# Last rows of a hybrid decoder step: gates in the one-hot rows, residual rows added by TensorE, sample rows spread over 64 partitions, tiles normed and stored one by one

## The chip, the core and the metric

The kernel runs on one core of a Trainium2 chip. The metric is the device time of one launch in microseconds. A core has TensorE (PE in the profile, its weight loads PEld), VectorE (DVE), ScalarE (ACT), GpSimd (POOL) and SyncE (SP), which here issues the large transfers; they run side by side, each in the order of its own queue, and wait for each other on semaphores.

## What is computed

One inference step of a decoder of two layers over 256 prompt rows and 8 sample rows of 1024 numbers, all in f32. The last sublayer is a mixture of eight experts, of which each row uses two, and the layer ends with a norm of each row:

```python
y = jnp.zeros_like(x)
for e in range(N_EXPERTS):
    y = y + swiglu(x, w_gu[e], w_down[e]) * combine[..., e:e + 1].astype(x.dtype)
...
hp = layer_norm(ALPHA * hp + fp, ln_g[i, 1], ln_b[i, 1])
hs = layer_norm(ALPHA * hs + fs, ln_g[i, 1], ln_b[i, 1])
```

`y_prompt` (256 x 1024) and `y_sample` (8 x 1024) are the last `hp` and `hs`; six states are further outputs, written long before the end.

## The kernel before

The rows stand in three tiles: tiles 0 and 1 are the 256 prompt rows, 128 to a tile on the partitions, and tile 2 is the 8 sample rows. The experts are run one after the other as jobs of up to 128 gathered rows. A job has 42 weight slots of 1 MB: SyncE loads a slot into `raw`, ScalarE rounds it to `high` (L352), VectorE subtracts to get `low` (L357), and TensorE multiplies with both (L2132 to L2136 for gate and up, L2161 and L2167 for down). In the loop over slots, `i` is the slot's number in its job.

A job's result of 128 rows is copied from PSUM banks 4 and 5 into `ysb`, half by ScalarE (L1017) and half by VectorE (L1631). All jobs but the last store it to DRAM. `acc` holds, for each tile, the residual (ALPHA times the row before the mixture); in the last expert VectorE adds the rows of each token's first and second expert that came from earlier jobs (L1602), gathered from DRAM and multiplied by the gate. The rows that come from the last job don't go through DRAM: `final_oh` (L1638) is a one-hot matrix of tokens by seats, TensorE transposes it (L2187), VectorE copies it into `final_ohT` (L1627), and after the last slot TensorE multiplies it with `ysb` (L2199), for the tiles in the order 2, 0, 1, two halves of 512 columns each, into the banks that `final_bank` names. All of these are f32 matmuls; the trace has two records (passes) for each.

VectorE then, for each tile in that order, adds the product times the gate to `acc` (L1662, one operation for each half), takes the statistics of each half (bn_stats, L1666) and combines them (bn_aggr, L1668). When all three are done, ScalarE takes Ln and Exp for 1/sqrt(var + eps) of all tiles (L1028, L1030), while VectorE runs (x - mean) * g over each tile (L1677) and then * rstd + b (L1682). Each tile of L1682 releases a store by SyncE (L515 for the sample rows, L517 for the prompt tiles of 512 KB each). GpSimd waits for the stores.

`Steps` is a counter with a semaphore: `step(instruction)` raises it, `step.wait()` waits for all that was counted.

Of the kernel before, what the change touches and what calls it, by code (L numbers as in the profile page):

```python
# [7 lines left out]
D = 1024  # L8
# [54 lines left out]
def hybrid_step(nc, x_prompt, x_sample, state_gdn_S, state_gdn_conv, state_sconv, ln_g, ln_b, gdn_w_in,  # L63
# [8 lines left out]
    with ExitStack() as ctx:  # L72
# [176 lines left out]
        gate_bm = place("gate_bm", [128, 3], at=region + 90 * D + 1568)  # L249
        zeros = place("zeros", [128, 256], at=zeros_at)  # L250
# [212 lines left out]
        def _(sp_):  # L463
# [48 lines left out]
            for tt in (2, 0, 1):  # L512
                sp_.wait_ge(y_ready, 1 + (0 if tt == 2 else tt + 1))
                if tt == 2:
                    sp_.dma_start(y_sample[:, 0, :], acc[0:NS, 2, :]).then_inc(y_out, 16)  # L515
                else:
                    sp_.dma_start(y_prompt[0, 128 * tt:128 * tt + 128, :], acc[:, tt, :]).then_inc(y_out, 16)  # L517
# [3 lines left out]
        def _(pool):  # L521
# [164 lines left out]
            pool.wait_ge(y_out, 48)  # L686
# [8 lines left out]
        def _(act):  # L695
# [331 lines left out]
            act.wait_ge(var_ready, 2)  # L1027
            act.activation(rstd_n[:, :], moments[:, :, 1], ACT.Ln, bias=eps[:, 1:2]).then_inc(log_ready, 1)  # L1028
            act.wait_ge(log_ready, 1)
            act.activation(rstd_n[:, :], rstd_n[:, :], ACT.Exp, scale=-0.5).then_inc(rstd_ready, 1)  # L1030
# [3 lines left out]
        def _(dve):  # L1034
# [569 lines left out]
            def expert(job, last, first=False):  # L1604
# [6 lines left out]
                for i in range(EXPERT_SLOTS):  # L1611
# [10 lines left out]
                    if i == EXPERT_SLOTS - 3:  # L1622
                        if not last:
                            gathered(job + 1)
                        else:
                            dve.wait_ge(ohT_psum, 1)
                            dve.tensor_copy(final_ohT[:, :], bank[2][:, 0:N]).then_inc(ohT_ready, 1)  # L1627
# [8 lines left out]
                    if last and i == 2:  # L1636
                        for tt in range(3):
                            ins = dve.tensor_scalar(final_oh[:, tt, :], seat[:, :], seat_b[:, tt:tt + 1], None, ALU.is_equal)  # L1638
                        ins.then_inc(oh_ready, 1)
                    if last and i in (20, 22, 24):  # L1640
# [15 lines left out]
            for i, tt in enumerate((2, 0, 1)):  # L1656
                p = 128 if tt < 2 else NS
                step.wait()
                for g in range(2):
                    dve.wait_ge(yrow_psum, 2 * i + g + 1)  # L1660
                    at = acc[0:p, tt, 512 * g:512 * g + 512]
                    step(dve.scalar_tensor_tensor(at, bank[final_bank(tt) + g][0:p, :], gate_ab[0:p, 1, tt:tt + 1], at,  # L1662
                                                  ALU.mult, ALU.add))
                step.wait()
# [563 lines left out]
```

## Time and profile before

| | us |
|---|---|
| median of 3 runs (1565.75 to 1566.30) | 1566.19 |
| profiled execution | 1567.19 |
| its span (first to last record on the core) | 1565.5 |
| PE busy | 1531.1 |
| DVE busy | 1279.2 |
| ACT busy | 1039.8 |

Times in the trace count from the start of the span. A group of instructions is given by line, engine, operation and tiles (out<-in), with its count, its busy time and the mean time of one. "idle before" is the time in which the engine did nothing just before them, with what ended it.

### The profile page before, as it was taken

Reading aid. Unit: us, or ns where it says so; the run is one execution under the profiler, and the core shown is the slowest. Engines: PE = TensorE matmul, PEld = TensorE weight load, DVE = VectorE, ACT = ScalarE, POOL = GpSimd, SP = SyncE. Lnnn points to the kernel's source line nnn. Section 1 sums busy time; section 2 is a strip of 40 time slices with the busy share of each in tenths; the row PEclk is TensorE's granted clock in tenths of the full one; section 3 lists DMA queues with packets and bytes.
Section 4 is the critical chain, followed back from the end, with each engine's and each line's share of the span. In section 5 each row is a group of like instructions: output and inputs, shape, how many; then the busy total and the mean of one; then the engine's idle time right before and its main releaser. Section 6 shows DMA issues by size and latency. Waiting matters only on the chain.

```text
span 1565.5 us, 23507 instructions
## 1 busy us (share of the span) xinstructions
PE 1531.1 (98%) x8904; PEld 1342.8 (86%) x8904; DVE 1279.2 (82%) x1285; ACT 1039.8 (66%) x967; POOL 104.2 (7%) x155
## 2 busy tenths in 40 slices
PE   8999999999999999999999999999999999999995
PEld 7899999999999998888888888888888888888883
DVE  6886555787446868999889889889889889889897
ACT  5874335676335447778778778778778778777772
POOL 3106000011000011000000000000000000003100
PEclk9999999999999999999999999999999999999998
DMA  9747605698545539999999999999999999999990
GB/s 290 241 138 275 236 15 188 202 300 283 188 162 190 188 110 373 376 380 383 386 376 374 386 375 373 389 373 378 389 373 371 391 373 377 387 378 373 411 399 28
DMA packets 227447, 476.67 MB, mean 304 GB/s; under 512 B 9692, under 2 KB 69100, under 8 KB 227081
## 3 DMA queue, kind: packets, MB, share of 16 engines
q1 hardware_dynamic: 216040, 435.66, 76.6%
q0 software_dynamic: 11344, 40.12, 7.5%
q8 instruction: 45, 0.74, 0.2%
q14 instruction: 18, 0.15, 0.0%
HBM read 449.74 MB, written 26.24 MB: 304 GB/s over the span
## 4 chain that ended last, share of the span: by engine, by line
PE 89%; DVE 5%; ACT 4%; issue 2%; DMA 0%; DVEq 0%; SPq 0%; ACTq 0%
PE bank L2136 13%; PE bank L2132 12%; PE bank L2133 12%; PE bank L392 12%; PE bank L2161 11%; PE bank L398 6%; PE bank L2167 5%; PE bank L1996 2%; DVE low L357 2%; ACT high L352 2%; PE bank L2144 2%; PE bank L1817 1%; DVE xf L1542 1%; PE bank L2001 1%; PE bank L1833 1%
## 5 line engine op out<-in xcount | busy, mean ns | idle before, releaser
L357 DVE TENSOR_TENSOR low<-raw,high 128x2048 fp32r<-128x2048 f32 x405 | 920.7, 2289 | 147.9 <-ACT high L352 145.3
L352 ACT ACTIVATE high<-raw 128x2048 fp32r<-128x2048 f32 x405 | 775.5, 1918 | 299.1 <-PE bank L2136 92.1
L2132 PE MATMUL bank<-high,xgh 128*128 128x512 f32 x896 | 353.8, 395 | 0.4 <-DVE xgl L1548 0.4
L2133 PE MATMUL bank<-high,xgl 128*128 128x512 f32 x896 | 349.5, 390 | 0.0
L2136 PE MATMUL bank<-low,xgh 128*128 128x512 f32 x896 | 241.3, 391 | 0.9 <-DVE low L357 0.5
L2136 PEld LDWEIGHTS bank<-low,xgh 128*128 128x128 f32 x896 | 167.5, 188 | 39.9 <-DVE low L357 4.6
L2132 PEld LDWEIGHTS bank<-high,xgh 128*128 128x128 f32 x896 | 168.3, 188 | 34.5 <-issue 0.5
L2133 PEld LDWEIGHTS bank<-high,xgl 128*128 128x128 f32 x896 | 168.3, 188 | 33.9
L392 PE MATMUL bank<-xhb,high 128*128 128x266 f32 (+1 forms) x752 | 158.0, 292 | 0.0
L392 PE MATMUL bank<-xlb,high 128*128 128x266 f32 (+1 forms) x752 | 155.0, 287 | 0.0
L2161 PE MATMUL bank<-high,hth 128*128 128x512 f32 x448 | 139.5, 392 | 0.0
L2161 PE MATMUL bank<-high,htl 128*128 128x512 f32 x448 | 138.2, 390 | 0.0
L392 PEld LDWEIGHTS bank<-xhb,high 128*128 128x128 f32 x752 | 119.1, 191 | 2.0 <-issue 1.8
L2167 PE MATMUL bank<-low,hth 128*128 128x512 f32 x448 | 119.9, 389 | 0.0
L392 PEld LDWEIGHTS bank<-xlb,high 128*128 128x128 f32 x752 | 118.9, 191 | 0.0
L398 PE MATMUL bank<-xhb,low 128*128 128x266 f32 (+1 forms) x752 | 100.4, 286 | 0.0
L2161 PEld LDWEIGHTS bank<-high,htl 128*128 128x128 f32 x448 | 84.1, 188 | 17.7
L2167 PEld LDWEIGHTS bank<-low,hth 128*128 128x128 f32 x448 | 84.1, 188 | 17.6
L2161 PEld LDWEIGHTS bank<-high,hth 128*128 128x128 f32 x448 | 82.9, 188 | 16.4
L398 PEld LDWEIGHTS bank<-xhb,low 128*128 128x128 f32 x752 | 95.7, 189 | 0.1
L1009 ACT ACTIVATE sgx<-bank 128x512 f32<-128x512 f32 x56 | 33.6, 600 | 39.4 <-PE bank L2136 39.3
L679 POOL TENSOR_TENSOR flag<-flag 128x1 f32<-128x1 f32 x1 | 3.4, 3352 | 838.2 <-DMA tok<-ysb 838.2
(417 smaller groups left out, 1554.8 us busy)
## 6 DMA issues: line engine op xcount, KB each, us to landing
raw<-in_moe_w_gu_dram SPq DMA_DIRECT2D x224, 1024.0 KB, 6.5
raw<-in_moe_w_down_dram SPq DMA_DIRECT2D x112, 1024.0 KB, 6.6
raw<-in_ffn_w_gu_dram SPq DMA_DIRECT2D x22, 1024.0 KB, 5.1
raw<-in_gdn_w_in_dram SPq DMA_DIRECT2D x16, 1024.0 KB, 8.7
tok<-zeros POOLq DMA_DIRECT2D x26, 512.0 KB, 18.1
raw<-in_sc_w_in_dram SPq DMA_DIRECT2D x12, 1024.0 KB, 5.0
raw<-in_ffn_w_down_dram SPq DMA_DIRECT2D x11, 1024.0 KB, 4.9
s<-in_state_gdn_S_dram POOLq DMA_DIRECT2D x8, 512.0 KB, 6.5
```

Of the source, the lines that this page charges most:

```text
L352: eng.activation(high[:, n % SPLIT, :], raw[:, n % RAW, :], ACT.Copy).then_inc(high_ready, 1)
L357: eng.tensor_tensor(low[:, n % RAW, :], raw[:, n % RAW, :], high[:, n % SPLIT, :].bitcast(F32), ALU.subtract).then_inc(low_ready, 1)
L392: pe.matmul(out[t], wh[:, k, f[t]], act_[:, k, :], start=k == 0 and act_ is act_h, stop=False)
L398: last = pe.matmul(out[t], wl[:, k, f[t]], act_h[:, k, :], start=False, stop=k == KT - 1)
L1009: act.activation(sgx[:, u % 2, :], bank[2 * (u % 2)][:, :], ACT.Silu).then_inc(sgx_ready, 1)
L1996: pe.matmul(bank[d][:, 0:N], wh[:, k, 128 * d:128 * d + 128], act_[:, f + k, :], start=f + k == 0 and act_ is hh, stop=False)
L2132: pe.matmul(out, xgh[:, 4 * kh + k, :], wh[:, k, :], start=kh + k == 0, stop=False)
L2133: pe.matmul(out, xgl[:, 4 * kh + k, :], wh[:, k, :], start=False, stop=False)
L2136: last = pe.matmul(out, xgh[:, 4 * kh + k, :], wl[:, k, :], start=False, stop=kh == 1 and k == 3)
L2144: last = pe.transpose(bank[6 + u % 2][:, 128 * q:128 * q + 128], hx[:, u % 2, 128 * q:128 * q + 128], idn)
L2161: pe.matmul(bank[4 + g][:, :], src[:, u % 2, hs], wh[:, k, 512 * g:512 * g + 512], start=u + kh + k == 0 and src is hth, stop=False)
L2167: last = pe.matmul(bank[4 + g][:, :], hth[:, u % 2, hs], wl[:, k, 512 * g:512 * g + 512], start=False, stop=u == UNITS - 1 and kh + k == 2)
```

## The change

The gate of the last job's expert is multiplied into the one-hot matrix `final_oh`, so the product of L2199 comes out gated. TensorE adds the residual: a matmul of the identity with `acc` goes into the same PSUM bank ahead of the product. VectorE takes statistics and the centred rows straight from PSUM. The order of the tiles becomes 0, 1, then the sample rows. The 8 sample rows of 1024 are laid out as 64 partitions of 128: `row_win` and `seat_win` are windows of 64 weight columns, shifted by one for each of eight blocks of 128 columns; eight matmuls of each kind build the rows in bank 0, and sixteen more spread the norm's g and b in bank 1. `same_row` sums a row's eight partitions, once for the mean and once for the variance. ScalarE takes Ln and Exp for each tile by itself. Tile 0 is finished and stored first, then the sample rows, then tile 1 in two halves of 512 columns.

```diff
--- before.py
+++ after.py
@@ -247,6 +247,16 @@
         part_a = place("part_a", [128, 3, EX], at=tab_at + 6048)
         seat_b = place("seat_b", [128, 3], at=region + 90 * D + 1536)
         gate_bm = place("gate_bm", [128, 3], at=region + 90 * D + 1568)
+        seat_win = place("seat_win", [128, 72], at=tab_at + 480)
+        row_win = place("row_win", [NS, 72], at=tab_at + 768)
+        same_row = place("same_row", [HEADS * NS, HEADS * NS], at=tab_at + 1056)
+        row_of = place("row_of", [HEADS * NS, NS], at=tab_at + 1312)
+        sstats = place("sstats", [HEADS * NS, 6], at=tab_at + 1344)
+        smom = place("smom", [HEADS * NS, 2], at=tab_at + 1376)
+        smean = place("smean", [HEADS * NS, 1], at=tab_at + 1408)
+        srstd = place("srstd", [HEADS * NS, 1], at=tab_at + 1440)
+        srows = place("srows", [HEADS * NS, 128], at=tab_at + 1472)
+        srow_g = place("srow_g", [HEADS * NS, 128], at=region + 24 * D)
         zeros = place("zeros", [128, 256], at=zeros_at)
         tok = nc.dram_tensor("tok", [JOBS + 2, CAP, D], F32).ap()
         tok_rows = tok.rearrange("j p d -> (j p) d")
@@ -509,12 +519,14 @@
                     down(UNITS - 1)
                 sp_.wait_ge(tiles_ready, 1)
                 sp_.reg_load(tiles, rounds_i[0:1, 0:1])
-            for tt in (2, 0, 1):
-                sp_.wait_ge(y_ready, 1 + (0 if tt == 2 else tt + 1))
-                if tt == 2:
-                    sp_.dma_start(y_sample[:, 0, :], acc[0:NS, 2, :]).then_inc(y_out, 16)
-                else:
-                    sp_.dma_start(y_prompt[0, 128 * tt:128 * tt + 128, :], acc[:, tt, :]).then_inc(y_out, 16)
+            sp_.wait_ge(y_ready, 1)
+            sp_.dma_start(y_prompt[0, 0:128, :], acc[:, 0, :]).then_inc(y_out, 16)
+            sp_.wait_ge(y_ready, 2)
+            sp_.dma_start(y_sample[:, 0, :].rearrange("b (d c) -> (b d) c", c=128), srows[:, :]).then_inc(y_out, 16)
+            for g in range(2):
+                gs = slice(512 * g, 512 * g + 512)
+                sp_.wait_ge(y_ready, 3 + g)
+                sp_.dma_start(y_prompt[0, 128:256, gs], acc[:, 1, gs]).then_inc(y_out, 16)
 
 
         @block.gpsimd
@@ -683,7 +695,7 @@
             for tt in (2, 0, 1):
                 gather_rows(1, tt, rows_b, b_in[tt])
 
-            pool.wait_ge(y_out, 48)
+            pool.wait_ge(y_out, 64)
             pool.wait_ge(hist_out, 48)
             pool.wait_ge(tail_out, 32)
             for i in range(2):
@@ -1024,10 +1036,15 @@
                 expert(job, False)
             expert(final, True)
             act.preload_act_table_set("natural_log_exp_and_others")
-            act.wait_ge(var_ready, 2)
-            act.activation(rstd_n[:, :], moments[:, :, 1], ACT.Ln, bias=eps[:, 1:2]).then_inc(log_ready, 1)
-            act.wait_ge(log_ready, 1)
-            act.activation(rstd_n[:, :], rstd_n[:, :], ACT.Exp, scale=-0.5).then_inc(rstd_ready, 1)
+            for tt in range(2):
+                act.wait_ge(var_ready, 2 + tt)
+                act.activation(rstd_n[:, tt:tt + 1], moments[:, tt, 1:2], ACT.Ln, bias=eps[:, 1:2]).then_inc(log_ready, 1)
+                act.wait_ge(log_ready, 1 + tt)
+                act.activation(rstd_n[:, tt:tt + 1], rstd_n[:, tt:tt + 1], ACT.Exp, scale=-0.5).then_inc(rstd_ready, 1)
+            act.wait_ge(yrow_psum, 8)
+            act.activation(srstd[:, :], bank[5][0:HEADS * NS, 1:2], ACT.Ln, bias=eps[0:HEADS * NS, 1:2]).then_inc(log_ready, 1)
+            act.wait_ge(log_ready, 3)
+            act.activation(srstd[:, :], srstd[:, :], ACT.Exp, scale=-0.5).then_inc(rstd_ready, 1)
 
 
         @block.vector
@@ -1624,7 +1641,11 @@
                             gathered(job + 1)
                         else:
                             dve.wait_ge(ohT_psum, 1)
-                            dve.tensor_copy(final_ohT[:, :], bank[2][:, 0:N]).then_inc(ohT_ready, 1)
+                            step(dve.tensor_copy(final_ohT[:, :], bank[2][:, 0:N]))
+                            step(dve.tensor_copy(seat_win[:, 0:64].rearrange("p (b d) -> p b d", d=8)[:, :, 7:8],
+                                                 bank[2][:, NP:N].rearrange("p (b o) -> p b o", o=1)))
+                            step.wait()
+                            dve.tensor_scalar(same_row[:, :], same_row[:, :], 1.0 / 8, None, ALU.mult).then_inc(ohT_ready, 1)
                     if i == EXPERT_SLOTS - 1:
                         dve.wait_ge(slot_used, done + (MOE0 + i + 1))
                         dve.wait_ge(y_stored, job * 16 + 16)
@@ -1635,8 +1656,18 @@
                         residual_rows((i - 12) // 4)
                     if last and i == 2:
                         for tt in range(3):
-                            ins = dve.tensor_scalar(final_oh[:, tt, :], seat[:, :], seat_b[:, tt:tt + 1], None, ALU.is_equal)
+                            ins = dve.tensor_scalar(final_oh[:, tt, :], seat[:, :], seat_b[:, tt:tt + 1], gate_ab[:, 1, tt:tt + 1],
+                                                    ALU.is_equal, ALU.mult)
                         ins.then_inc(oh_ready, 1)
+                    if last and i == 14:
+                        step(dve.memset(seat_win[:, :], 0.0))
+                        step(dve.memset(row_win[:, :], 0.0))
+                        step(dve.tensor_reduce(row_of[:, :], ident[0:64, 0:64].rearrange("p (b d) -> p b d", d=8), X, ALU.add))
+                        step.wait()
+                        step(dve.tensor_copy(row_win[:, 0:64].rearrange("p (b d) -> p b d", d=8)[:, :, 7:8],
+                                             ident[0:NS, 0:NS].rearrange("p (b o) -> p b o", o=1)))
+                        step(dve.tensor_copy(same_row[:, :].rearrange("p (b d) -> p b d", d=8),
+                                             row_of[:, :].rearrange("p (b o) -> p b o", o=1).to_broadcast([64, NS, 8])))
                     if last and i in (20, 22, 24):
                         tt = (2, 0, 1)[(i - 20) // 2]
                         p = 128 if tt < 2 else NS
@@ -1653,34 +1684,50 @@
                 expert(job, False)
             step.wait()
             expert(final, True)
-            for i, tt in enumerate((2, 0, 1)):
-                p = 128 if tt < 2 else NS
+
+            def row_moments(tt):
+                for g in range(2):
+                    dve.wait_ge(yrow_psum, 2 * tt + g + 1)
+                    step(dve.bn_stats(stats[:, tt, g, :], bank[final_bank(tt) + g][:, :]))
                 step.wait()
+                dve.bn_aggr(moments[:, tt, :], stats[:, tt, :, :].rearrange("p g s -> p (g s)")).then_inc(var_ready, 1)
+
+            def centred(tt):
+                dve.wait_ge(var_ready, 2 + tt)
                 for g in range(2):
-                    dve.wait_ge(yrow_psum, 2 * i + g + 1)
-                    at = acc[0:p, tt, 512 * g:512 * g + 512]
-                    step(dve.scalar_tensor_tensor(at, bank[final_bank(tt) + g][0:p, :], gate_ab[0:p, 1, tt:tt + 1], at,
-                                                  ALU.mult, ALU.add))
-                step.wait()
-                for g in range(2):
-                    step(dve.bn_stats(stats[:, tt, g, :], acc[:, tt, 512 * g:512 * g + 512]))
-                step.wait()
-                ins = dve.bn_aggr(moments[:, tt, :], stats[:, tt, :, :].rearrange("p g s -> p (g s)"))
-                if tt == 1:
-                    ins.then_inc(var_ready, 1)
-                else:
-                    step(ins)
-            step.wait()
-            dve.wait_ge(var_ready, 2)
-            dve.wait_ge(vec_in, 64)
-            for tt in (2, 0, 1):
-                step(dve.scalar_tensor_tensor(acc[:, tt, :], acc[:, tt, :], moments[:, tt, 0:1], vec_g[:, :],
-                                              ALU.subtract, ALU.mult))
-            step.wait()
+                    gs = slice(512 * g, 512 * g + 512)
+                    step(dve.scalar_tensor_tensor(acc[:, tt, gs], bank[final_bank(tt) + g][:, :], moments[:, tt, 0:1], vec_g[:, gs],
+                                                  ALU.subtract, ALU.mult))
+
+            def finished(tt, gs):
+                dve.scalar_tensor_tensor(acc[:, tt, gs], acc[:, tt, gs], rstd_n[:, tt:tt + 1], vec_b[:, gs],
+                                         ALU.mult, ALU.add).then_inc(y_ready, 1)
+
+            x_rows = bank[0][0:HEADS * NS, 0:128]
+            row_moments(0)
+            row_moments(1)
+            centred(0)
+            dve.wait_ge(yrow_psum, 5)
+            step(dve.bn_stats(sstats[:, :], x_rows))
+            step.wait()
+            dve.bn_aggr(smom[:, :], sstats[:, :]).then_inc(var_ready, 1)
             dve.wait_ge(rstd_ready, 2)
-            for tt in (2, 0, 1):
-                dve.scalar_tensor_tensor(acc[:, tt, :], acc[:, tt, :], rstd_n[:, tt:tt + 1], vec_b[:, :],
-                                         ALU.mult, ALU.add).then_inc(y_ready, 1)
+            finished(0, slice(0, D))
+            dve.wait_ge(yrow_psum, 7)
+            step(dve.tensor_copy(srow_g[:, :], bank[1][0:HEADS * NS, 0:128]))
+            step(dve.tensor_copy(smean[:, :], bank[4][0:HEADS * NS, 0:1]))
+            step.wait()
+            step(dve.tensor_tensor(smom[:, 0:1], smom[:, 0:1], smean[:, :], ALU.subtract))
+            step.wait()
+            dve.scalar_tensor_tensor(smom[:, 1:2], smom[:, 0:1], smom[:, 0:1], smom[:, 1:2], ALU.mult, ALU.add).then_inc(var_ready, 1)
+            centred(1)
+            step(dve.scalar_tensor_tensor(srows[:, :], x_rows, smean[:, 0:1], srow_g[:, :], ALU.subtract, ALU.mult))
+            step.wait()
+            dve.wait_ge(rstd_ready, 4)
+            dve.scalar_tensor_tensor(srows[:, :], srows[:, :], srstd[:, 0:1], bank[1][0:HEADS * NS, 128:256],
+                                     ALU.mult, ALU.add).then_inc(y_ready, 1)
+            for g in range(2):
+                finished(1, slice(512 * g, 512 * g + 512))
 
 
         @block.tensor
@@ -2192,12 +2239,40 @@
                 expert(job, False)
             expert(final, True)
             pe.wait_ge(ohT_ready, 1)
+
+            def residual(tt, g):
+                pe.matmul(bank[final_bank(tt) + g][:, :], idn, acc[:, tt, 512 * g:512 * g + 512], start=True, stop=False)
+
+            def weighted(tt, g):
+                pe.matmul(bank[final_bank(tt) + g][:, :], final_ohT[:, 128 * tt:128 * tt + 128], ysb[:, 512 * g:512 * g + 512],
+                          start=False, stop=True).then_inc(yrow_psum, 1)
+
+            for g in range(2):
+                residual(0, g)
             pe.wait_ge(y_sb, final * 2 + 4)
-            for i, tt in enumerate((2, 0, 1)):
-                n_tok = 128 if tt < 2 else NS
-                for g in range(2):
-                    pe.matmul(bank[final_bank(tt) + g][0:n_tok, :], final_ohT[:, 128 * tt:128 * tt + n_tok],
-                              ysb[:, 512 * g:512 * g + 512], start=True, stop=True).then_inc(yrow_psum, 1)
+            for g in range(2):
+                weighted(0, g)
+            for g in range(2):
+                residual(1, g)
+                weighted(1, g)
+
+            def sample_rows(out, win, rows):
+                for d in range(KT):
+                    last = pe.matmul(out, win[:, 7 - d:71 - d], rows[:, 128 * d:128 * d + 128], start=d == 0, stop=d == KT - 1)
+                return last
+
+            x_rows = bank[0][0:HEADS * NS, 0:128]
+            for d in range(KT):
+                ds = slice(128 * d, 128 * d + 128)
+                pe.matmul(x_rows, row_win[:, 7 - d:71 - d], acc[0:NS, 2, ds], start=d == 0, stop=False)
+                last = pe.matmul(x_rows, seat_win[:, 7 - d:71 - d], ysb[:, ds], start=False, stop=d == KT - 1)
+            last.then_inc(yrow_psum, 1)
+            pe.wait_ge(vec_in, 64)
+            sample_rows(bank[1][0:HEADS * NS, 0:128], row_win, vec_g[0:NS, :])
+            sample_rows(bank[1][0:HEADS * NS, 128:256], row_win, vec_b[0:NS, :]).then_inc(yrow_psum, 1)
+            for i in range(2):
+                pe.wait_ge(var_ready, 4 + i)
+                pe.matmul(bank[4 + i][0:HEADS * NS, 0:2], same_row[:, :], smom[:, :], start=True, stop=True).then_inc(yrow_psum, 1)
 
 
 # ---- launch: one core; inputs and outputs as the reference has them ----
```

## Rows read from the trace of the kernel before

**Rows 1.** The page: TensorE's busy share; granted clock in 40 slices.
```profile
PE 1531.1 (98%) x8904; PEld 1342.8 (86%) x8904; DVE 1279.2 (82%) x1285; ACT 1039.8 (66%) x967; POOL 104.2 (7%) x155
...
PEclk9999999999999999999999999999999999999998
```
**Rows 2.** The chain of waits from 1530 to 1566: start, us, what.
```profile
1542.32 1.90 PE bank L2199 x4
...
1544.24 0.75 DVE acc L1662
...
1549.59 1.42 DVE acc L1662 x2
...
1558.85 1.20 DVE acc L1682
```
**Rows 3.** The timeline of the end: start, us, engine, line, what, count.
```profile
1540.38 1.07 PE L2167 MATMUL bank<-low,hth 128*128 128x512 f32 x4
...
1541.58 0.69 DVE L1631 COPY ysb<-bank 128x512 f32<-128x512 f32 x1 [3.88 <-PE bank L2167]
...
1542.32 5.51 PE L2199 MATMUL bank<-ysb,final_ohT 128*8 128x512 f32 x12 [0.88 <-DVE ysb L1631]
...
1543.45 1.53 DVE L1662 SCALAR_TENSOR_TENSOR acc<-bank,gate_ab,acc 8x512 f32<-8x512 f32 x2 [1.19 <-PE bank L2199]
...
1558.88 1.53 SPq L517 DMA_DIRECT2D out_dram<-acc  x2
```
**Rows 4.** DMA from 1558 to 1566 in 40 slices: busy tenths, GB/s.
```profile
DMA  0072000039999989999991000000000000000000
GB/s 0 0 102 41 21 0 0 0 143 410 410 451 389 430 369 492 389 410 471 389 430 62 0 0 0 0 0 0 0 0 0 0 0 0 0 0 0 0 0 0
```
**Rows 5.** Groups by form, whole span: busy us, mean ns, idle before.
```profile
L2109 PE MATMUL bank<-onehot,xn 128*128 128x128 f32 x48 | 5.6, 277 | 0.0
...
L2109 PEld LDWEIGHTS bank<-onehot,xn 128*128 128x128 f32 x48 | 5.4, 192 | 0.5 <-DVE onehot L1508 0.5
...
L1666 DVE BATCH_NORM_STATS2 stats<-acc 128x6 f32<-128x512 f32 x6 | 3.9, 685 | 0.1
L1682 DVE SCALAR_TENSOR_TENSOR acc<-acc,rstd_n,vec_b 128x1024 f32<-128x1024 f32 x3 | 3.7, 1282 | 0.0
...
L1441 DVE BATCH_NORM_STATS2 quarters<-bank 128x6 f32<-128x256 f32 x8 | 3.0, 414 | 0.8 <-PE bank L2035 0.8
...
L1248 DVE SCALAR_TENSOR_TENSOR Vn<-bank,nbe,Vn 128x128 f32<-128x128 f32 x8 | 2.2, 342 | 2.0 <-PE bank L1891 2.0
...
L1668 DVE BATCH_NORM_AGGREGATE moments<-stats 128x2 f32<-128x12 f32 x3 | 0.6, 208 | 0.1
...
L1627 DVE COPY final_ohT<-bank 128x264 f32<-128x264 f32 x1 | 0.4, 426 | 0.0
...
L1533 DVE TENSOR_TENSOR most<-most 128x1 f32<-128x1 f32 x1 | 0.2, 159 | 0.0
...
L1028 ACT ACTIVATE rstd_n<-moments,eps 128x3 f32<-128x3 f32 x1 | 0.3, 297 | 9.1 <-DVE moments L1668 9.1
```
**Rows 6.** Waits in the last expert, 1425 to 1541: total, times, longest us.
```profile
DVE low L357 <- ACT high L352: 4.8, 10, 0.8
...
PEld bank L2136 <- DVE low L357: 0.4, 1, 0.4
```
**Rows 7.** VectorE's timeline in the last expert.
```profile
1469.33 2.29 DVE L357 TENSOR_TENSOR low<-raw,high 128x2048 fp32r<-128x2048 f32 x1 [0.42 <-ACT high L352]
1472.05 2.29 DVE L357 TENSOR_TENSOR low<-raw,high 128x2048 fp32r<-128x2048 f32 x1 [0.43 <-ACT high L352]
```
**Rows 8.** Windows: busy us of each engine, granted clock, DMA share, GB/s.
```profile
583.00:589.00 6.00, 5.64 (x49) 5.46 (x49) 4.43 (x24) 0.63 (x2) 2.66 (x3) 1.00 0.25 104
1547.50:1551.00 3.50, 0.34 (x1) 0.00 (x0) 3.40 (x6) 0.00 (x0) 0.00 (x0) 1.00 0.00 0
...
1552.40:1560.00 7.60, 0.00 (x0) 0.00 (x0) 7.47 (x7) 0.50 (x2) 0.00 (x0) 0.50 0.06 19
```

More of the change, by code:

```diff
@@ L1679, in _ @@
-            step.wait()
-            dve.wait_ge(rstd_ready, 2)
-            for tt in (2, 0, 1):
-                dve.scalar_tensor_tensor(acc[:, tt, :], acc[:, tt, :], rstd_n[:, tt:tt + 1], vec_b[:, :],
-                                         ALU.mult, ALU.add).then_inc(y_ready, 1)
+                    gs = slice(512 * g, 512 * g + 512)
+                    step(dve.scalar_tensor_tensor(acc[:, tt, gs], bank[final_bank(tt) + g][:, :], moments[:, tt, 0:1], vec_g[:, gs],
+                                                  ALU.subtract, ALU.mult))
@@ new lines, in _ @@
+            dve.wait_ge(rstd_ready, 2)
+            finished(0, slice(0, D))
+            dve.wait_ge(yrow_psum, 7)
+            step(dve.tensor_copy(srow_g[:, :], bank[1][0:HEADS * NS, 0:128]))
+            step(dve.tensor_copy(smean[:, :], bank[4][0:HEADS * NS, 0:1]))
+            step.wait()
+            step(dve.tensor_tensor(smom[:, 0:1], smom[:, 0:1], smean[:, :], ALU.subtract))
+            step.wait()
+            dve.scalar_tensor_tensor(smom[:, 1:2], smom[:, 0:1], smom[:, 0:1], smom[:, 1:2], ALU.mult, ALU.add).then_inc(var_ready, 1)
```

## The prediction

> **What bounds the kernel now.** I read the page first. TensorE is busy for 98% of the span, at the full clock in all of the 40 slices but the last [rows 1]: the kernel is bound by TensorE until its last microseconds, and those are another stage. The change acts almost only there. Then the chain of waits over the end [rows 2]: it runs through the copy into ysb and the first products of L2199, and from 1544.24 to 1560.05 through VectorE alone, so this stage is VectorE's chain, and the stores behind it. The timeline gives starts and spacings [rows 3]: twelve records of L2199 are six f32 matmuls of two passes, 0.43 us a pass; the first result is seen by VectorE at 1543.45, 1.13 us after its first pass began at 1542.32, that is 0.86 of streaming and 0.27 of drain and semaphore. The DMA view of the last 8 us (slices of 0.2) [rows 4]: the data of the two 512 KB stores, issued at 1558.88 and 1560.07, flow from 1559.6 without a hole to about 1562.35 at some 420 GB/s; the span ends at 1565.5, so 3.15 us follow the last byte.
>
> **The change in the expert stage.** It adds VectorE work in the last expert (i == 14: two memsets, a reduction, two copies, all on 72 columns or fewer; about 0.8 us at 0.16 for the smallest operation and 0.001 a column [rows 5]) and two instructions behind the copy into final_ohT, about 0.4 us. In the last expert VectorE waits 4.8 us in all for ScalarE's splits, and TensorE waited for VectorE's low half 0.4 us in all [rows 6]. The work of i == 14 falls at 1468.9, between two splits; the next two of them waited 0.42 and 0.43 us [rows 7], which takes up the 0.8. The other two fall in the 3.9 us in which VectorE waits for the last slot [rows 3]. I cost both at 0. Without that cover they cost at most 1.2 us, which goes into the range. The gate in final_oh is a second operation of the same instructions: 0. ScalarE's pairs (0.30 or less each [rows 5]) are small; the last is checked below.
>
> **The end, step by step.** TensorE first, since the change gives it far more to do ahead of VectorE.
>
> 1. *Residuals ahead of the product.* The four L2167 passes began at 1540.38 [rows 3], 0.23 apart, so the array is free at 1541.29. Two residual matmuls are four passes of 0.43, to 1543.01. ysb is there at 1542.28 [rows 3], so 0.7 us of them is on the path: the first product is seen at 1543.01 + 1.13 = 1544.14, the second at 1545.00.
> 2. *Second tile.* Residual and product alternate, 0.86 each: seen at 1546.72 and 1548.44, array free at 1548.17.
> 3. *Sample rows.* 16 f32 matmuls of 128 columns, 32 passes. The nearest row is L2109, 48 passes with 5.6 us busy, 0.117 each [rows 5]; a quarter of the 512-column pass is 0.107. The weights here have 64 columns, not 128; I take 0.110. 3.5 us, to 1551.7, seen at 1551.96.
> 4. *The norm's vectors spread over the rows.* 32 passes more, 3.5 us, to 1555.2. The first same_row product (two passes of two columns) is seen at about 1555.6.
>
>    A rule of the Trainium skill bears on the price of a pass. The rows show a load of 128 columns at 0.19 us of its own, and a period of 0.117 with it [rows 5]. "TensorE: Matmul & The Clock Gate", in its part on LDWEIGHTS, says that a load takes about its columns over 1.2 GHz, however many rows it has; as an estimate from it, 53 ns for 64 columns, which would hide under 0.107 of streaming: 6.8 us for the 64 passes by the page, 7.5 by the row.
>
> VectorE against this:
>
> 5. Tile 0: two bn_stats of 0.685 from 1544.14 and 1545.00, aggregate 0.21 [rows 5]: 1545.9. Tile 1: from 1546.72 and 1548.44, done at 1549.37; these waits are for TensorE. centred(0) is two operations in the form of L1662, 1.42 us a pair [rows 2]: 1550.85.
> 6. It waits for the sample rows until 1551.96. bn_stats of 128 columns: 512 cost 0.685 and 256 cost 0.414 [rows 5], so 0.28; aggregate 0.2: 1552.5. finished(0) is 1.28 [rows 5]: 1553.8. The first 512 KB store starts there, 6 us before VectorE ends, moves its data in 1.3 us and is out of the way. What comes later in VectorE's queue stands behind its next wait, yrow_psum 7, though centred(1) doesn't need it: idle from 1553.8 to 1555.6.
> 7. Copy of 128 columns 0.29 (0.16 for the smallest operation, 0.43 for 264 columns), copy of one column 0.15, two tiny operations at 0.16 each [rows 5]: 1556.4. centred(1) 1.42: 1557.85. Two operations on 64x128 at 0.34 each (L1248 [rows 5]): 1558.5. ScalarE's last pair needs the second same_row product (1556.9) and 0.6 us: 1557.5, hidden.
> 8. finished(1) in halves, again a pair at 1.42: 1559.9. Before, the last operation ended at 1560.05. Gain on VectorE: 0.15 us. It saved about 8.2 us (three gate pairs 1.42 x 3, the sample tile's two 1024-column operations 1.20 x 2, its statistics 1.5); that went into waits for TensorE of 0.7, 0.15, 0.8, 1.0, 1.1 and 1.8 us, 1.9 of small operations, and 0.6 because halves cost 1.42 where a whole cost 1.20.
> 9. *The stores.* The last is 256 KB, behind another 256, instead of 512 behind 512. Issued at 1559.2 and 1559.9, first data 0.7 us after issue as before, 0.63 us each at 420 GB/s: last byte at 1561.3 instead of 1562.35. Then the same 3.15 us: 1564.5. The 64 sample rows of 512 B are issued at 1558.5, ahead of both; the 32 KB before took under 0.7 us [rows 4].
>
>    By the rows the stores give 0.9 us beyond VectorE's 0.15. The Trainium skill, "DMA: Bandwidth & Descriptors", on where the 2 us of a transfer go, has it as 2.0 us fixed, mostly the receipt of the last write, plus bytes over 436 GB/s; as an estimate from it the last store lands 2.6 us after issue instead of 3.2, and the stores give 0.6. This trace has 3.15 us after the last byte, part of it the end of the program.
>
> Sum: 1564.5 against 1565.5, **1.0 us less**. The profiled execution took 1567.19 for its span of 1565.5; the median of the runs is 1566.19, so 1565.2.
>
> **Bounds of the unknown costs.** Pass: 0.107 gives -0.2 us; the upper bound is the 0.19 of a 128-column load [rows 5] if nothing hides it, +5.1. Residual matmuls: the form of L2199, +-0.1. Stores: no gain (+0.9) to the full 1.05. Small operations of step 7: 0.13 each (-0.2) to 0.25 (+0.4). Expert stage: 0 to +1.2.
>
> **The rivals.**
>
> *The short passes are bound by their loads (slower).* Place: the 64 passes of steps 3 and 4; VectorE's last 4.3 us stand behind them, so each microsecond counts in full. For it: the load row has 0.19, more than the pass that it feeds, and the weights alternate between 8 and 128 rows. Against it: L2109 has the same 0.19 and a period of 0.117, and 64 columns are fewer. At 0.19 the span is 1569.6, the median 1570.3. It decides (over +3.1) from 0.174 us a pass.
>
> *The clock falls during the short passes (slower, mostly within the bound).* TensorE was idle from 1547.9 on before, and the granted clock was 1.00 until 1551 and 0.50 from 1552.4: 2.4 and then 1.2 GHz [rows 8]. If short passes didn't hold it and the 32 of step 4 ran at the lower level, they would take 3.5 us more: 1568.7. Against it: L2109's stretch is at 1.00 [rows 8] with the same kind of pass. The Trainium skill's page on TensorE and its clock gate ties half rate to an array that has been idle; here it is never idle before 1555.2.
>
> *TensorE is not the limit (faster).* If a short pass took half, 0.055, step 4 would end 3.5 us earlier and VectorE would follow: 1561.7. Against it: no f32 row of 128 columns lies under 0.107. It decides from about 0.077.
>
> *The stores are hidden anyway.* If the last bytes land as far behind VectorE's end as with 512 KB, 0.15 is all: 1566.0, no change.
>
> **How the numbers follow.** 0.2%, 3.1 us, is about what a measurement of this kernel can tell from no change. As worked out, within the small bounds: 0.61, at 1565.2. Stores without gain, or the expert stage not covered: 0.16 (1566.0 to 1567.4). Clock: 0.07 (1568.7). Loads: 0.09 (to 1570.3). Faster passes: 0.07 (down to 1561.7). The range 1562.8 to 1568.7 cuts the far ends of the last two. Faster by over 0.2%: 0.08. Slower, from the loads and a clock that falls for more than 37 passes: 0.11. Within: 0.81.
>
> **What would show it.** Right: eight matmuls of 0.86 from 1541.3; 64 short passes over about 7 us to 1555.2; VectorE idle 1.8 us before the copy into srow_g with TensorE as releaser; last operation near 1559.9, last byte near 1561.3. Wrong: short passes 0.15 or more apart, a clock under 1.00 before 1555, a wait of TensorE for low above 0.4 us in the last expert, or a longer stretch between the last byte and the end.

## The result and the profile after

The changed kernel took 1572.98 us in the median of 7 runs (1570.38 to 1575.72), the kernel before 1566.30 us (7 runs). The ratio is 1.0037, 95% interval 1.0026 to 1.0048 (the two medians alone give 1.0043): 0.4% slower, outside the range and against the forecast. The profiled execution took 1573.17 us, with a span of 1571.1.

The page of the changed kernel, its busy times and granted clock, against [rows 1]:

```profile
PE 1546.9 (98%) x8976; PEld 1354.8 (86%) x8976; DVE 1273.4 (81%) x1292; ACT 1040.9 (66%) x971; POOL 102.2 (7%) x155
...
PEclk9999999999999999999999999999999999999997
```

VectorE lost 5.8 us of work, as meant, and TensorE gained 15.8. The last slice's clock digit is 7 instead of 8. The timeline of the end, against [rows 2, 3]:

```profile
1540.39 1.88 PE L2244 MATMUL bank<-acc,ident 128*128 128x512 f32 x4
...
1543.17 0.70 DVE L1691 BATCH_NORM_STATS2 stats<-bank 128x6 f32<-128x512 f32 x1 [1.79 <-PE bank L2247]
...
1547.35 0.43 PE L2267 MATMUL bank<-acc,row_win 8*64 8x128 f32 x2
...
1547.71 0.43 PE L2268 MATMUL bank<-ysb,seat_win 128*64 128x128 f32 x2
...
1548.07 0.43 PE L2267 MATMUL bank<-acc,row_win 8*64 8x128 f32 x2
...
1551.67 0.69 PE L2268 MATMUL bank<-ysb,seat_win 128*64 128x128 f32 x2
...
1552.29 0.69 PE L2267 MATMUL bank<-acc,row_win 8*64 8x128 f32 x2
...
1554.76 3.67 PE L2261 MATMUL bank<-vec_g,row_win 8*64 8x128 f32 x16
...
1554.87 0.29 DVE L1711 BATCH_NORM_STATS2 sstats<-bank 64x6 f32<-64x128 f32 x1 [5.19 <-PE bank L2268]
...
1561.77 0.37 PE L2275 MATMUL bank<-smom,same_row 64*64 64x2 f32 x2
1562.18 0.28 DVE L1717 COPY srow_g<-bank 64x128 f32<-64x128 f32 x1 [5.65 <-PE bank L2275]
...
1564.84 1.40 DVE L1703 SCALAR_TENSOR_TENSOR acc<-acc,rstd_n,vec_b 128x512 f32<-128x512 f32 x2
```

A short matmul (two passes, so x2) of the sample rows starts every 0.36 us at first, then every 0.62; the sixteen take 7.4 us instead of the 3.5 forecast. The sixteen for the norm's vectors take 7.0, one each 0.44, instead of 3.5. VectorE waits 5.19 us for the first lot and 5.65 for the second. Windows of the same execution (busy us of PE, PEld, DVE, ACT, POOL, then granted clock, DMA share, GB/s):

```profile
1547.40:1550.60 3.20, 3.20 (x20) 1.66 (x19) 2.18 (x4) 0.50 (x2) 0.00 (x0) 1.00 0.00 0
1550.60:1550.80 0.20, 0.20 (x3) 0.18 (x2) 0.00 (x0) 0.00 (x0) 0.00 (x0) 0.96 0.00 0
1550.80:1551.00 0.20, 0.20 (x2) 0.00 (x0) 0.00 (x0) 0.00 (x0) 0.00 (x0) 0.50 0.00 0
...
1554.80:1561.80 7.00, 7.00 (x34) 6.67 (x33) 1.64 (x3) 0.00 (x0) 0.00 (x0) 0.50 0.18 75
```

The granted clock goes from 1.00 to 0.50 (2.4 to 1.2 GHz) at 1550.8, while TensorE is recorded as busy all the time. So there are two losses: a price of 0.36 instead of about 0.22 at the full clock, and a clock that fell in the middle.

To compare executions, the table below uses two distances within each trace: from the start of the first residual matmul (before: 1541.29, where the last slot's passes end) to VectorE's last end, and from there to the end of the span. Each trace is a single execution; the ratios are of 4 to 11 runs against before in the same rounds.

| kernel | to VectorE's end, us | from there to the span's end, us | ratio to before, 95% interval |
|---|---|---|---|
| before | 18.75 | 5.46 | 1 |
| changed | 25.85 | 4.86 | 1.0037 (1.0026 to 1.0048) |
| e1 grouped | 19.06 | 4.90 | 1.0005 (0.9995 to 1.0015) |
| e2 128-row windows | 18.46 | 4.82 | 0.9995 (0.9986 to 1.0005) |
| e3 128-column windows | 27.77 | 4.89 | 1.0062 (1.0045 to 1.0079) |
| e4 sample rows not spread | 17.54 | 4.68 | 0.9989 (0.9980 to 0.9999) |
| e5 e2, centring earlier | 17.80 | 4.85 | 0.9993 (0.9984 to 1.0002) |
| e6 e2, tile 1 whole | 18.33 | 5.36 | 1.0005 (0.9996 to 1.0014) |
| e7 vectors by GpSimd's transfers | 14.96 | 6.29 | 0.9991 (0.9982 to 1.0000) |
| e8 e2, 8-row vector matmuls, twice | 26.28 | 4.83 | one run: 1573.50 us |
| e9 e2, vector matmuls twice | 21.96 | 4.84 | one run: 1572.59 us |
| e10 vectors by SyncE's transfers | 14.96 | 4.53 | 0.9980 (0.9971 to 0.9989) |
| e11 e4, sample tile last | 17.53 | 4.51 | 0.9989 (0.9980 to 0.9998) |

### The profile page after: what moved, and what is told of

The parts are those of the page before. It is cut to its first block, busy times and chain, and to the rows that moved or that the text cites. A ratio compares the mean times of both kernels' runs of the same rounds, so it can differ in the third digit from the quotient of the medians.

```text
span 1571.1 us, 23659 instructions
## 1 busy us (share of the span) xinstructions
PE 1546.9 (98%) x8976; PEld 1354.8 (86%) x8976; DVE 1273.4 (81%) x1292; ACT 1040.9 (66%) x971; POOL 102.2 (7%) x155
## 4 chain that ended last, share of the span: by engine, by line
PE 90%; DVE 4%; ACT 4%; issue 2%; DMA 0%; DVEq 0%; SPq 0%; ACTq 0%
PE bank L2183 13%; PE bank L2179 12%; PE bank L2180 12%; PE bank L402 11%; PE bank L2208 11%; PE bank L408 6%; PE bank L2214 5%; PE bank L2043 2%; DVE low L367 2%; ACT high L362 2%; PE bank L2191 2%; PE bank L1864 1%; DVE xf L1559 1%; PE bank L2048 1%; PE bank L1880 1%
```

## The experiments

**e1: the same matmuls, grouped by the rows of their weights.**

```diff
-                pe.matmul(x_rows, row_win[:, 7 - d:71 - d], acc[0:NS, 2, ds], start=d == 0, stop=False)
-                last = pe.matmul(x_rows, seat_win[:, 7 - d:71 - d], ysb[:, ds], start=False, stop=d == KT - 1)
+                pe.matmul(x_rows, row_win[:, 7 - d:71 - d], acc[0:NS, 2, 128 * d:128 * d + 128], start=d == 0, stop=False)
+            for d in range(KT):
+                last = pe.matmul(x_rows, seat_win[:, 7 - d:71 - d], ysb[:, 128 * d:128 * d + 128], start=False, stop=d == KT - 1)
```

> The changed kernel, but the eight row_win matmuls (weights of 8 rows) come before the eight seat_win matmuls (128 rows) instead of alternating with them. Theory A (each change between 8-row and 128-row weights stalls TensorE, 0.15 us at the high clock): a matmul of the sample rows takes 0.21 to 0.23 us instead of 0.36, all sixteen 3.5 us instead of 7.3. If the stalls are also what let the clock fall (A1), it stays at 1.00 until the end of the 32 matmuls and the kernel takes about 7.4 us less than the changed one, about 1 us less than before. If short matmuls of this kind lose the clock in any order (A2), it falls at the same place, about 3.5 us after the last 512-column matmul, and the gain over the changed kernel is about 4 us. Theory W (64-column weights are the trouble, whatever the order): 0.36 a matmul and the time of the changed kernel.

**e2: the same order, weights of 128 rows throughout.** `row_win` gets 120 rows of zeros, and the moving side is the whole tile.

```diff
-        row_win = place("row_win", [NS, 72], at=tab_at + 768)
+        row_win = place("row_win", [128, 72], at=tab_at + 768)
-                pe.matmul(x_rows, row_win[:, 7 - d:71 - d], acc[0:NS, 2, ds], start=d == 0, stop=False)
+                pe.matmul(x_rows, row_win[:, 7 - d:71 - d], acc[:, 2, ds], start=d == 0, stop=False)
-            sample_rows(bank[1][0:HEADS * NS, 0:128], row_win, vec_g[0:NS, :])
-            sample_rows(bank[1][0:HEADS * NS, 128:256], row_win, vec_b[0:NS, :]).then_inc(yrow_psum, 1)
+            sample_rows(bank[1][0:HEADS * NS, 0:128], row_win, vec_g)
+            sample_rows(bank[1][0:HEADS * NS, 128:256], row_win, vec_b).then_inc(yrow_psum, 1)
```

> The changed kernel with row_win on 128 partitions (zero below row 8), so that all 32 short matmuls load 128-row weights of 64 columns, in the changed kernel's alternating order. Theory A: no change of row count, so 0.21 to 0.23 us a matmul, as when grouped, and the same time as the grouped one. Theory W: 0.36 a matmul, the time of the changed kernel. If the clock depends on how many rows of the array are fed (R), it holds here at 1.00 to the end of the short matmuls, and falls in the grouped kernel, whose last 16 load 8 rows.

**e3: alternating rows, weights of 128 columns.**

```diff
-        seat_win = place("seat_win", [128, 72], at=tab_at + 480)
-        row_win = place("row_win", [NS, 72], at=tab_at + 768)
+        seat_win = place("seat_win", [128, 136], at=region)
+        row_win = place("row_win", [NS, 136], at=region + 576)
```

> The changed kernel with windows of 128 columns instead of 64 (the upper 64 output rows are not used), 8-row and 128-row weights still alternating. Theory A: still 0.36 us a matmul at the high clock or a little more, no gain. Theory W: 0.23 us a matmul, as the rows gathered with 128-column weights earlier in the kernel, and at least 2 us less than the changed kernel.

TensorE's timeline in e1, then in e2, then in e3:

```profile
1550.70 1.96 PE L2266 MATMUL bank<-acc,row_win 8*64 8x128 f32 x16
...
1552.59 1.96 PE L2268 MATMUL bank<-ysb,seat_win 128*64 128x128 f32 x16
```
```profile
1548.23 0.38 PE L2268 MATMUL bank<-ysb,seat_win 128*64 128x128 f32 x2
1548.45 0.38 PE L2267 MATMUL bank<-acc,row_win 128*64 128x128 f32 x2
1548.66 0.38 PE L2268 MATMUL bank<-ysb,seat_win 128*64 128x128 f32 x2
...
1550.63 1.91 PE L2261 MATMUL bank<-vec_g,row_win 128*64 128x128 f32 x16
```
```profile
1549.13 0.48 PE L2267 MATMUL bank<-acc,row_win 8*128 8x128 f32 x2
...
1549.55 0.49 PE L2268 MATMUL bank<-ysb,seat_win 128*128 128x128 f32 x2
1549.96 0.48 PE L2267 MATMUL bank<-acc,row_win 8*128 8x128 f32 x2
```

Grouped, eight matmuls start 1.89 us after the eight before them, 0.236 each; with 128 rows and the alternating order of two tiles they are 0.22 apart. With 128-column windows and alternating rows they are 0.42 apart. So it is not the 64 columns (theory W falls): each change between weights of 8 and of 128 rows costs 0.14 us at 2.4 GHz (0.36 - 0.218), 0.2 with 128 columns (0.42 - 0.218). The grouped ones agree: one such change in eight matmuls adds 0.14 / 8 = 0.018 to 0.218, and 0.236 was measured. Theory A holds. The Trainium skill ("TensorE: Matmul & The Clock Gate", the mechanism of row and column tiling) says that a weight load overlaps the matmuls in flight only where the row group differs; the same part also lets a load into a background weight buffer be pulled ahead. The trace doesn't agree with the first: loads with the same rows were hidden (0.109 a pass, against 0.107 for a quarter of the 512-column pass). Loads that changed between 8 and 128 rows were not; these two share their first rows, and no run here has weights on separate rows.

The clock in e1, then in e2, in windows as above:

```profile
1554.50:1556.40 1.90, 1.90 (x19) 1.90 (x19) 1.64 (x3) 0.00 (x0) 0.00 (x0) 1.00 0.00 0
1556.40:1557.40 1.00, 1.00 (x12) 1.00 (x11) 0.00 (x0) 0.00 (x0) 0.00 (x0) 1.00 0.28 115
1557.40:1558.30 0.90, 0.90 (x8) 0.60 (x5) 0.00 (x0) 0.00 (x0) 0.00 (x0) 0.74 1.02 419
```
```profile
1550.60:1554.20 3.60, 3.60 (x34) 3.44 (x32) 1.64 (x3) 0.00 (x0) 0.00 (x0) 1.00 0.24 99
1554.20:1556.00 1.80, 0.56 (x5) 0.38 (x4) 1.40 (x6) 0.30 (x2) 0.00 (x0) 1.00 0.23 93
```

In e1 it falls late, among the last 8-row matmuls, so neither A1 (1.00 to the end) nor A2 (a fall at the same place) came as written, and its time was not 1 us under before; in e2 it doesn't fall before the short matmuls are done. That left two reasons for the fall in the changed kernel, the stalls at the changes and the few rows. Two kernels take them apart.

**e8 and e9: twice as many matmuls for the norm's vectors, weights of 8 or of 128 rows, no alternation.** Both are e2 with this block, which writes the same sums twice; e9 has `row_win, vec_g` and `row_win, vec_b` without the slices.

```diff
+            for _ in range(2):
+                sample_rows(bank[1][0:HEADS * NS, 0:128], row_win[0:NS, :], vec_g[0:NS, :])
+                last = sample_rows(bank[1][0:HEADS * NS, 128:256], row_win[0:NS, :], vec_b[0:NS, :])
+            last.then_inc(yrow_psum, 1)
```

> The kernel with 128-row windows (e2), but the 16 matmuls that spread the norm's vectors load weights of 8 rows and are done twice (32 matmuls, 64 passes, the second time over the same bank). TensorE is busy without a gap and changes the row count once. If the clock falls because few rows of the array are fed, it falls within these 32 matmuls, 0.22 us each turning into 0.44. If it was the stalls at each change of row count that let it fall, it stays at 1.00 and the 32 take 7.0 us.

> The same with weights of 128 rows in all of the 32 matmuls done twice. By both theories the clock stays at 1.00 for all of them, 0.22 us each, 7.0 us in all. If short matmuls as such lose the clock after long enough (e2 had only 7 us of them), it falls here as in the kernel with 8 rows.

TensorE's timeline in e8, its windows, and the windows of e9:

```profile
1550.89 1.96 PE L2261 MATMUL bank<-vec_g,row_win 8*64 8x128 f32 x16
1552.68 2.67 PE L2261 MATMUL bank<-vec_b,row_win 8*64 8x128 f32 x16
1555.15 3.62 PE L2261 MATMUL bank<-vec_g,row_win 8*64 8x128 f32 x16
```
```profile
1550.80:1552.60 1.80, 1.80 (x18) 1.71 (x17) 1.57 (x3) 0.00 (x0) 0.00 (x0) 1.00 0.00 0
...
1553.60:1554.40 0.80, 0.80 (x7) 0.80 (x5) 0.00 (x0) 0.00 (x0) 0.00 (x0) 0.54 0.97 399
1554.40:1562.00 7.60, 7.60 (x37) 7.38 (x35) 0.00 (x0) 0.00 (x0) 0.00 (x0) 0.50 0.06 23
```
```profile
1554.10:1557.60 3.50, 3.50 (x34) 3.50 (x33) 1.64 (x3) 0.00 (x0) 0.00 (x0) 1.00 0.23 90
1557.60:1561.10 3.50, 3.50 (x34) 3.42 (x32) 0.00 (x0) 0.00 (x0) 0.00 (x0) 1.00 0.17 64
```

With 8-row weights and TensorE busy without a gap, the clock fell all the same, and eight matmuls went from 1.8 to 3.4 us; with 128-row weights it held through 10.5 us of short matmuls. So a run of matmuls with weights of 8 rows lost the clock without any stall. Whether the stalls alone would was not tried, nor any count between 8 and 128, and each of the two kernels was executed once. The store of tile 0 moves its data just where the clock falls in e8 (DMA share 0.97) and in e1, but it isn't the reason: at the fall in the changed kernel the DMA share is 0.00, and in e2 and e9 the same store passes at a clock of 1.00.

**e4: only the spreading undone.** The sample rows are a third tile of 8 partitions, with its own residual and product matmuls (512 columns), statistics and one store.

```diff
-            x_rows = bank[0][0:HEADS * NS, 0:128]
-            for d in range(KT):
...
+            for tt in (1, 2):
+                for g in range(2):
+                    residual(tt, g)
+                    weighted(tt, g)
```

> The changed kernel with only the spreading of the sample rows undone: they are handled as a third tile of 8 partitions (residual and product by TensorE, two halves of 512), stored as one piece; gates in the one-hot rows, residuals by TensorE, tiles one by one and the two half stores remain. All theories that put the loss into the short matmuls: last VectorE operation about 2 us earlier than in the kernel before, time 1 to 3 us below before, 8 to 10 below the changed kernel. A rival, that the residual matmuls ahead of the product or the half stores cost it: at or above the time of the kernel before.

Its median was 1564.77 us, 0.1% below before (1566.77 in the same rounds) and 8.2 us below the changed kernel's; by the two ratios, 7.5. So the loss is in the spreading. The rest of the change is worth 1.2 us on VectorE's chain (17.54 against 18.75; 2 were expected) and 0.8 behind it.

**e11: e4, with the sample tile behind tile 1, its store last.** The calls for tile 2 in VectorE's program move behind `finished(1, ...)`, its store behind the halves.

> The kernel e4 (sample rows as a third tile of 8 partitions), with the sample tile handled behind tile 1, so that the last store is its 32 KB. VectorE's work is the same, 17.5 us from the free array to its end; the last 256 KB are stored 4 us earlier. If the bytes of the last store count, 0.6 us under e4: about 1564. If it is the receipt and the end of the program alone, no difference.

0.2 us less behind VectorE's end, and the same ratio as e4. The 0.6 didn't come.

**e5: e2, with centred(1) ahead of the wait.**

```diff
+            centred(1)
             dve.wait_ge(yrow_psum, 7)
...
-            centred(1)
```

> The kernel with 128-row windows (e2), with centred(1) moved ahead of VectorE's wait for yrow_psum 7. In e2 VectorE was idle 2.03 us there and then spent 1.39 us on centred(1) behind it. If this wait is what sets the end, all of the 1.39 us comes off: last VectorE operation 17.1 us after the array is free instead of 18.5, time 1.4 us under e2. Rival: ScalarE's last pair, now uncovered, holds back the sample rows (it ended at 1556.15 in e2, against centred(1)'s end at 1556.6); then only 0.5 to 1.0 us.

VectorE in e5:

```profile
1557.09 0.34 DVE L1727 SCALAR_TENSOR_TENSOR srows<-srows,srstd,bank 64x128 f32<-64x128 f32 x1 [0.70 <-ACT srstd L1047]
```

0.66 us of the 1.39 came off (18.46 to 17.80); the other 0.7 is a new wait for ScalarE's last pair, which the centring had covered. That was the rival. The ratios of e5 and e2 can't be told apart, so this rests on the traces.

**e6: e2, tile 1 finished and stored whole.**

```diff
-            for g in range(2):
-                finished(1, slice(512 * g, 512 * g + 512))
+            finished(1, slice(0, D))
```

> The kernel with 128-row windows (e2), but tile 1 is finished in one operation of 1024 columns and stored as one piece of 512 KB, as before the change. VectorE then ends 0.15 us earlier. By the prediction's step 9 the store should cost 0.9 us less the 0.25 that it no longer has another store ahead: last byte 0.6 us later behind VectorE's end. By the traces of e2 and of the kernel before (4.82 and 5.45 us from VectorE's end to the span's end) 0.6 as well. Rival: stores in halves bring nothing, as the end waits for the receipt and the issue of one more transfer: no difference, or this one faster by the 0.15. If the 0.35 us more between span and time that all changed kernels show comes from the additional store, it goes here too.

VectorE ended 0.13 us earlier and 0.54 us more followed it (5.36 against 4.82). The halves are worth that behind VectorE's end, less than the 0.9 of the prediction. The ratios of e2 and e6 overlap, so this rests on one profiled execution of each, and on before's 5.46 and the changed kernel's 4.86.

**e7 and e10: the norm's vectors by 16 transfers of 4 KB instead of 32 passes.** Both also finish tile 0 and centre tile 1 before the waits, and store the sample rows last. In e7 GpSimd issues the transfers in the last expert; in e10 SyncE does, behind the last weight slot's load:

```diff
+            for to, src in ((srow_g, ln_g), (srow_b, ln_b)):
+                for b in range(NS):
+                    sp_.dma_start(to[HEADS * b:HEADS * b + HEADS, :], src[1, 1].rearrange("(d c) -> d c", c=128)).then_inc(x_in, 16)
             sp_.wait_ge(y_ready, 1)
```

> The kernel with 128-row windows (e2), and the norm's vectors reach the 64 partitions by 16 small transfers during the last expert instead of by 32 passes of TensorE; tile 0 is finished before the wait for the sample rows, tile 1's centring before the wait for the mean, and the sample rows are stored last. If waits for TensorE's short matmuls are what remained in e2: VectorE's last operation 15.3 us after the array is free (18.5 in e2, 18.8 in the kernel before), span about 4 us under e2's, time 1561 to 1562, faster than before by 0.3%. Rival: the small transfers' issue or the additional loads delay the last expert, or the waits only move to ScalarE's last pair: less than 2 us under e2.

> The kernel e7, but SyncE issues the 16 small transfers, after the last weight slot's load (SyncE had nothing to do for some 30 us then), instead of GpSimd during the last expert. In e7 VectorE ended 15.0 us after the array was free, as forecast, but the last expert lost time (ScalarE waited 13.6 us for weight loads, 1.1 in the kernel with 128-row windows) and 6.3 us followed VectorE's end instead of 4.8. If the collision with the weight loads and a late fetch of GpSimd's longer program cost this, both go: 15.0 us to VectorE's end and 4.8 behind it, time 1562 to 1563, 0.9970 to 0.9980 of the kernel before. Rival: the 4.4 us between the last landing and the end come from the sample rows' store being last; then 6.3 us stay behind VectorE's end and the time is about 1564.

The "1.1" in e10's text is a slip: ScalarE waited 5.2 us for weight loads in e2's last expert, 1.4 in the changed kernel's. The waits in e7's last expert, then in e10's, and the row of the DMA view (1555 to 1565) that e7 has and e10 has not:

```profile
ACT high L363 <- DMA raw<-in_moe_w_gu_dram: 9.4, 11, 2.1
...
ACT high L363 <- DMA raw<-in_moe_w_down_dram: 4.2, 5, 1.2
...
PEld bank L2191 <- DVE low L368: 2.6, 4, 0.9
```
```profile
ACT high L363 <- DMA raw<-in_moe_w_gu_dram: 1.3, 2, 0.6
...
ACT high L363 <- DMA raw<-in_moe_w_down_dram: 1.2, 2, 0.8
...
PEld bank L2190 <- DVE low L368: 0.4, 1, 0.4
```
```profile
q14 instruction: 1, 0.01, 0.3%
```

Both ended VectorE's chain at 14.96 us, 3.8 under before (15.3 expected of e7). e7 gave much of it back: 1.5 us more than in e2 followed VectorE's end, and TensorE's weight loads waited 2.6 us for low halves in the last expert. With the transfers in SyncE's idle time neither is there, and e10 took 1562.47 us against 1566.36: 0.2% faster than before, the best of all. The guess that the store order made e7's tail falls, since e10 has the same order. The last store of e7 landed at about 1559.3, the one packet of an instruction queue moved at about 1560.5, and the span ended at 1563.8; in e10 2.7 us lie between the last landing and the end, without such a packet. That this fetch made the tail fits, but was not shown.

Whether the small transfers also held up the weight loads stays open. ScalarE's waits for weight loads in the last expert differ widely between executions without them: none in e5, 6.7 us in e4 and 9.4 in e6, against 13.6 in e7, and 5.6 of the 13.6 came after 1478, some 13 us behind the landing of the last small transfer. TensorE was busy for 113.72 of the 115 us from 1425 in e7, for 114.54 in e2 and e6 and for 115.00 in e10, so 0.8 us is what this one execution lost more than those. The longer tail (6.29 against 4.53) is by itself as large as the difference of the two ratios, 1.7 us.

## Why the prediction was wrong

**The expert stage (cost 0): right.** VectorE waited 4.4 us for ScalarE in the last expert (4.8 before), TensorE 0.4 for a low half as before, and the five operations of i == 14 took 0.5 us.

**Steps 1, 2 and 5: right.** The first product was seen 2.78 us after the array was free (2.85 forecast), and the sample rows' matmuls began 6.96 us after it (6.88 forecast).

**Steps 3 and 4 failed: the price of a short pass.** 0.110 us was taken from L2109, whose 48 passes all load 128 rows. The text saw that the weights here alternate between 8 and 128 rows, and let the row of L2109 speak against it, though that row has no alternation. It held that the clock stays up as long as the array is never idle; the trace after, and e8 without any change of the row count in its last 32 short matmuls, show it fall with TensorE recorded as busy. Against 0.218 a matmul (e2), the sixteen of step 3 lost about 2.3 us to changes of the row count (16 at 0.14) and the rest of their 3.9, 1.6, to the clock (7.4 - 3.5 - 2.3), and the sixteen of step 4 lost 3.5 to the clock: 7.4 us, which is also what e2 gives back (25.85 - 18.46). So VectorE waited for the sample rows until 14.48 us after the array was free, not 10.67 (step 6). Its chain came 7.2 us longer than forecast (25.85 against 1559.9 - 1541.3 = 18.6). With 0.3 less from the stores (step 9) and 0.35 outside the span, that is 7.9 over the forecast of 1565.2; the median lies 7.8 over it.

Both slower rivals named the place, and each had a part. The first put the price on the load's own 0.19: step 3 cost 0.18 a pass at the full clock, but the passes of step 4, whose loads all have 8 rows, show no such price (0.112 at the full clock in e8's first eight matmuls, 1.79 us). The second expected the clock to fall in step 4 only, and its 3.5 us came there exactly; it put this down to short passes as such, which e9 contradicts. Each alone stayed at 1570.3 or under; they came together. e2, where the row count never changes, and e1, where it changes only three times, show the forecast's chain: 18.46 and 19.06 against 18.6. The forecast's 0.110 a pass was right for weights of one row count. (The rival of faster passes was priced too high, which changed nothing here: by the steps VectorE waited 1.1 and 1.8 us for the short passes, so it could gain 2.9, not 3.5.)

**Steps 7 and 8: right in size.** From the copy into srow_g to VectorE's end 4.1 us, 4.3 forecast. centred(1) stood behind the wait for yrow_psum 7 as described; moved ahead of it (e5), 0.66 of its 1.39 us came back, since ScalarE was late next.

**Step 9: mis-sized.** 0.6 us behind VectorE's end instead of 0.9: 5.46 to 4.86. The DMA view of the changed kernel from 1560 to 1572 (slices of 0.3), against [rows 4]:

```profile
GB/s 0 0 0 0 0 0 0 0 0 0 0 0 0 0 0 0 0 0 0 0 75 34 362 416 376 423 171 0 0 0 0 0 0 0 0 0 0 0 0 0
```

The last byte moved at about 1567.9, 1.7 us behind VectorE's end (1566.24), where the forecast had 1.4 and before has 2.3; the stretch from there to the span's end was 3.2, as forecast. The 0.6 that followed, as an estimate, from the Trainium skill's formula ("DMA: Bandwidth & Descriptors", on where the 2 us of a transfer go; the page fitted it to transfers that GpSimd issues, these are SyncE's) was the better of the two, though of its 2.6 us from issue to landing the trace shows 2.2. And 0.35 us more lies outside the span: time less span is 1.7 us in the median of the runs of before, and 2.0 to 2.1 in those of the changed kernel and of all others with more than one run but e6, e4 without the spreading among them. In e6, with three stores like before, it is 2.8, and six of its 11 runs have 2.8 to 3.8, so the additional store is not the reason, and e6's time says little of its stores. The cause is open.

The runs of the changed kernel are spread over 5.3 us; those of e4 and of e10 over 3.5 and 4.7, and those of before, by round, over 3.5 to 5.0. The mean granted clock of a run goes with its time: 0.995 in the three fastest of the changed kernel and 0.992 in the slowest, 0.993 to 0.994 in the runs of before over 1569 us and 0.994 to 0.996 in its others. A clock that falls at another moment would do this; no experiment tied one to the other.

## What to carry to other kernels

Price a short matmul from a row with the same sequence of weights, not only the same shape: a change in the number of weight rows cost 0.14 us each time, and filling the small operand with zeros to the same 128 rows removed it without any cost in passes (0.109). Look at the granted clock where TensorE is recorded as busy: matmuls with 8-row weights lost it, those with 128-row weights kept it. When VectorE's work is moved to TensorE behind the last large matmul, count what stands in front of each wait: even with all passes at their forecast price the spreading of the sample rows brought nothing (e2 0.9995, e4 without it 0.9989). Data that only has to be laid out differently came cheaper by small transfers in a queue's idle time: e10, at 0.9980, was the fastest kernel (e2 0.9995; their intervals just touch). Part of its gain is the other order of VectorE's work, of which only the 0.66 us of e5 was measured by itself.

## What the runs showed of the hardware

Weight loads of 64 columns hid under passes of 0.109 us when the row count stayed, and not when it changed (0.36 a matmul of two passes at 2.4 GHz, 0.62 at 1.2, against 0.218 and 0.44 without a change). The granted clock went to 0.50 with TensorE recorded as busy throughout, on 8-row weights (e8), and stayed at 1.00 through 10.5 us of the same matmuls with 128-row weights (e9; one execution each). A last store of 256 KB instead of 512 ended the span 0.54 us sooner behind VectorE's last operation (4.82 in e2, 5.36 in e6) and 0.6 in the changed kernel (4.86, before 5.46).
